# Twelve early rows instead of eight, and half of the weights' low parts on GpSimd

## The reference: what is computed

```python
def peer(h, w_pq, sub_keys, u_tab, v_tab):
    qr = (h @ w_pq).reshape(b, t, 8, 2, 128)                       # queries: 2048 x 2048 weights
    sc = einsum('bthpd,hpnd->bthpn', qr, sub_keys)                 # 8 heads x 2 x 128 scores
    s_top, i_top = top_k(sc, 16)
    cand = s_top[..., 0, :, None] + s_top[..., 1, None, :]
    c_top, c_pos = top_k(cand.reshape(b, t, 8, 256), 16)           # 16 experts for each head
    expert = i0 * 128 + i1                                         # one of 16384
    g = softmax(c_top)
    a = gelu(einsum('bthkd,btd->bthk', u_tab[expert], h))
    return einsum('bthk,bthkd->btd', g * a, v_tab[expert])
```

## Time and profile before

| | us |
|---|---|
| median of 3 runs | 1524.09 (1523.74 to 1526.22) |
| the profiled execution, in all | 1527.39 |
| its span, first to last instruction | 1525.4 |
| PE busy in the span | 1448.7 (95%) |
| VectorE busy | 1153.4 (76%) |
| GpSimd busy | 428.1 (28%) |

### The profile page before, as it was taken

One profiled execution on the slowest core, in us unless ns is written; L12 is line 12 of the kernel. 1 busy time (PEld: TensorE's weight loads), 2 busy tenths in 40 slices (PEclk: granted clock), 3 DMA queues, 4 the chain that ended last, 5 costly groups with the idle time before them and its releaser, 6 DMA issues.

```text
span 1525.4 us, 21815 instructions
## 1 busy us (share of the span) xinstructions
PE 1448.7 (95%) x7977; PEld 1099.6 (72%) x7977; DVE 1153.4 (76%) x1797; ACT 486.7 (32%) x1402; POOL 428.1 (28%) x422
## 2 busy tenths in 40 slices
PE   8999999999999999999989999998887999999995
PEld 6767888888899999999989999973333344444442
DVE  5425688576686899998377777787666898888988
ACT  6646656764654200000144444466000000000000
POOL 2020000000001332223111111135554566666661
PEclk9999999999999999999999999999999999999998
DMA  9764544637679899999999999999999999999996
GB/s 346 276 133 114 164 134 140 206 129 249 199 241 375 339 412 422 421 422 421 422 421 422 420 423 421 422 410 418 418 416 416 392 382 402 403 391 359 405 400 231
DMA packets 115527, 516.23 MB, mean 338 GB/s; under 512 B 26112, under 2 KB 28288, under 8 KB 63312
## 3 DMA queue, kind: packets, MB, share of 16 engines
q0 software_dynamic: 57776, 294.93, 48.9%
q1 hardware_dynamic: 47888, 154.09, 28.3%
q10 hardware_dynamic: 9792, 66.35, 10.5%
HBM read 628.91 MB, written 3.41 MB: 415 GB/s over the span
## 4 chain that ended last, share of the span: by engine, by line
PE 49%; DMA 26%; DVE 18%; issue 3%; ACT 1%; POOL 1%; another core or an unknown queue 0%; DVEq 0%; POOLq 0%; ACTq 0%; SPq 0%
PE ps L1589 12%; PE ps L1634 10%; DMA acts<-in_v_tab,acts 9%; PE ps L1373 6%; PE ps L1378 6%; PE ps L1375 6%; DMA late<-in_u_rows,sel 5%; DVE ps L1195 3%; DMA late<-in_v_tab,acts 3%; DVE late L1186 3%; DMA late<-in_u_tab 2%; PE ps L1395 2%; DVE acts L1186 2%; DMA raw<-in_w_pq 2%; DMA acts<-in_u_rows,sel 2%
## 5 line engine op out<-in xcount | busy, mean ns | idle before, releaser
L871 DVE TENSOR_TENSOR w_lo<-raw,w_hi 128x512 fp32r<-128x512 f32 (+1 forms) x288 | 187.6, 682 | 132.4 <-ACT w_hi L564 131.1
L1589 PE MATMUL ps<-acts,late 128*128 128x128 f32 x1984 | 233.9, 277 | 9.0 <-DMA late<-in_u_tab 7.2
L1589 PEld LDWEIGHTS ps<-acts,late 128*128 128x128 f32 x1984 | 227.1, 193 | 13.1 <-ACT acts L777 6.6
L1589 PE MATMUL ps<-acts,raw 128*128 128x128 f32 x1984 | 231.8, 276 | 2.6 <-DMA raw<-in_u_tab 2.3
L1589 PEld LDWEIGHTS ps<-acts,raw 128*128 128x128 f32 x1984 | 225.5, 192 | 5.3 <-DMA raw<-in_u_tab 3.1
L564 ACT ACTIVATE w_hi<-raw 128x512 fp32r<-128x512 f32 (+1 forms) x288 | 169.4, 621 | 89.3 <-PE ps L1378 35.5
L1634 PE MATMUL ps<-raw,acts 128*128 128x512 f32 x352 | 163.2, 617 | 18.8 <-DMA raw<-in_v_tab,acts 17.5
L1195 DVE SCALAR_TENSOR_TENSOR ps<-acts,sel,ps 128x2048 f32<-128x2048 f32 x63 | 148.3, 2355 | 20.1 <-DMA acts<-in_v_tab,acts 13.8
L1195 DVE SCALAR_TENSOR_TENSOR ps<-late,sel,ps 128x2048 f32<-128x2048 f32 x63 | 148.3, 2355 | 17.6 <-DMA late<-in_v_tab,acts 10.4
L1634 PE MATMUL ps<-late,acts 128*128 128x512 f32 x336 | 150.9, 598 | 10.2 <-DMA late<-in_v_tab,acts 9.5
L1634 PE MATMUL ps<-acts 128*128 128x512 f32 x336 | 150.2, 597 | 5.7 <-DMA acts<-in_v_tab,acts 4.9
(11 more groups left out here) (225 smaller groups left out, 1949.0 us busy)
## 6 DMA issues: line engine op xcount, KB each, us to landing
raw<-in_w_in SPq DMA_DIRECT2D x72, 512.0 KB, 4.4
raw<-in_u_tab SPq DMA_DIRECT2D x32, 1024.0 KB
late<-in_u_tab SPq DMA_DIRECT2D x32, 1024.0 KB
raw<-in_u_tab ACTq DMA_DIRECT2D x30, 1024.0 KB
late<-in_u_tab ACTq DMA_DIRECT2D x30, 1024.0 KB
raw<-in_w_o SPq DMA_DIRECT2D x32, 512.0 KB, 3.7
raw<-in_w_pq SPq DMA_DIRECT2D x32, 512.0 KB, 4.7
acts<-in_u_tab SPq DMA_DIRECT2D x4, 1024.0 KB, 9.1
```

The lines of the kernel that those rows point to most:

```text
L871: V.tensor_tensor(wlo[slot_no][:, 0:w], raw[j % NRAW][:, half * w:half * w + w], whi[slot_no][:, 0:w].bitcast(F32), ALU.subtract).then_inc ...
L1589: ins = mm(ps[:, q, 0:N_DN], unit[:, k * P:k * P + P], hF[:, k, :], start=k == 0, stop=k == KD - 1)
```

## The change

GpSimd makes the low part of the second (odd) piece of each tile from tile 8 on, 24 in all, counted on a semaphore of its own (`odd_lo_done`); VectorE makes the first ones. TensorE, and SyncE before it reloads a buffer, wait for the counts of both. VectorE does twelve row products in the stage (`R_FRONT`), placed by `ROW_AT` after its low parts of tiles 17, 17, 19, 21, 21, 23, 25, 25, 27, 29, 29 and 31; GpSimd's gathers stand at `GATHER_AT`, after its low parts of tiles 14, 15, 18, 18, 20, 22, 22, 24, 26, 26, 28 and 30. During the first top-16 choice VectorE makes a low part at every other step. Expert units 3 and 2 are fetched after the first and second half of `w_o`'s tiles; units 0 and 1 stay where they were. The constants that count rows later on are each raised by four, so that at every later place VectorE and GpSimd stand four rows further.

```diff
-        ROWS_U = 88
-        R_FRONT, R_MORE, ROWS_PICKED = 8, 46, 39
+        ROWS_U = 92
+        R_FRONT, R_MORE, ROWS_PICKED = 12, 50, 43
+        SHARED = 16
+        ROW_AT = [17 + 2 * (2 * r // 3) for r in range(R_FRONT)]
+        GATHER_AT = [14, 15] + [at + 1 for at in ROW_AT[:-2]]
...
-        ROWS_SB = 81
+        ROWS_SB = 85
...
             for group in range(2):
                 with sp.Fori(0, D // 512) as n:
...
+                sp.wait_ge(y_mm, 8 * group + 8)
+                first_unit(3 - group)
...
+                for u in range(4 * first, 4 * end):
+                    sp.wait_ge(lo_done, 2 * B_PQ + SHARED + u + 1 - NRAW - SHARED // 2)
+                    sp.wait_ge(odd_lo_done, u + 1 - NRAW - SHARED // 2)
+                    sp.dma_start(raw[u % NRAW], io["w_pq"][u * P:u * P + P, :]).then_inc(raw_ready[u % NRAW], 16)
...
             first_unit(1)
-            query_weights(4, 5)
-            first_unit(2)
-            query_weights(5, 6)
-            first_unit(3)
-            query_weights(6, 8)
+            query_weights(4, 8)
...
-            gathers(0, R_FRONT + 6)
+            gathered = 0
+            for u in range(SHARED // 2, U_PQ):
+                pool.wait_ge(hi_done, 2 * (B_PQ + u) + 2)
+                part = (2 * u + 1) % NPART
+                nc.gpsimd.tensor_tensor(wlo[part][:, :], raw[u % NRAW][:, PIECE:2 * PIECE], whi[part][:, :].bitcast(F32), ALU.subtract).then_inc(odd_lo_done, 1)
+                end = sum(at <= u for at in GATHER_AT)
+                gathers(gathered, end)
+                gathered = end
+            gathers(gathered, R_FRONT + 6)
...
-                    split_lo_half(B_PQ + lo_halves[0] // 2, lo_halves[0] // 2, lo_halves[0] % 2)
-                    lo_halves[0] += 1
+                    split_lo_half(B_PQ + lo_halves[0] // 2, lo_halves[0] // 2, 0)
+                    lo_halves[0] += 2
...
             while lo_halves[0] < 2 * U_PQ:
-                for _ in range(4):
-                    weights_low()
-                if rows_done[0] < R_FRONT - 1:
-                    next_row()
+                weights_low()
+                next_row(sum(at < lo_halves[0] // 2 for at in ROW_AT) - rows_done[0])
             next_row(R_FRONT - rows_done[0])
...
-                pe.wait_ge(lo_done, 2 * B_PQ + piece + 1)
+                if piece < SHARED:
+                    pe.wait_ge(lo_done, 2 * B_PQ + piece + 1)
+                elif half:
+                    pe.wait_ge(odd_lo_done, (piece - SHARED + 1) // 2)
+                else:
+                    pe.wait_ge(lo_done, 2 * B_PQ + SHARED + (piece - SHARED) // 2 + 1)
```

More of the change, by code:

```diff
@@ L229, in build_block @@
         raw_ready = [sem(f"raw_ready{i}") for i in range(NRAW)]
-        hi_done, lo_done, piece_used = sem("hi_done"), sem("lo_done"), sem("piece_used")
+        hi_done, lo_done, odd_lo_done, piece_used = sem("hi_done"), sem("lo_done"), sem("odd_lo_done"), sem("piece_used")
         xT_in = [sem(f"xT_in{i}") for i in range(KD // 2)]
@@ L403, in _, with u_unit, first_unit @@
             wo = io["w_o"].rearrange("(k p) n -> p k n", p=P)
+            def u_unit(v):
+                return io["u_tab"][ds(v * P, P), :]
+            def first_unit(j):
+                sp.dma_start(first_units[j], u_unit(j)).then_inc(first_in[j], 16)
             for group in range(2):
@@ L408, in _ @@
                         load(n * 4 + (B_WO + 16 * group + j), j, wo[:, k:k + 2, ds(n * 512, 512)])
-            def u_unit(v):
-                return io["u_tab"][ds(v * P, P), :]
+                sp.wait_ge(y_mm, 8 * group + 8)
+                first_unit(3 - group)
             def query_weights(first, end):
[L413 to L418, removed]
+                if first < 3:
+                    with sp.Fori(first, end) as i:
+                        for j in range(4):
+                            load(i * 4 + (B_PQ + j), j, io["w_pq"][ds(i * (4 * P) + j * P, P), :])
+                    return
+                for u in range(4 * first, 4 * end):
+                    sp.wait_ge(lo_done, 2 * B_PQ + SHARED + u + 1 - NRAW - SHARED // 2)
+                    sp.wait_ge(odd_lo_done, u + 1 - NRAW - SHARED // 2)
+                    sp.dma_start(raw[u % NRAW], io["w_pq"][u * P:u * P + P, :]).then_inc(raw_ready[u % NRAW], 16)
             query_weights(0, 3)
@@ L424, in _ @@
             first_unit(1)
-            query_weights(4, 5)
-            first_unit(2)
-            query_weights(5, 6)
-            first_unit(3)
-            query_weights(6, 8)
+            query_weights(4, 8)
             for j in range(2):
-                sp.wait_ge(lo_done, 2 * (B_U + 2 * j + 1) - 2 * (NRAW - 1))
+                sp.wait_ge(lo_done, 2 * B_PQ + SHARED + U_PQ - SHARED // 2 - 2 + 2 * j)
+                sp.wait_ge(odd_lo_done, U_PQ - SHARED // 2 - 2 + 2 * j)
                 sp.dma_start(ring[j], u_unit(NRING + j)).then_inc(unit_in[j], 16)
@@ L1224, in row_numbers, with low_by_turns @@
                 V.scalar_tensor_tensor(idx[:, cols], slot[:, 0, cols], float(NKEY), slot[:, 1, cols], ALU.mult, ALU.add).then_inc(idx_ready, 1)
+            calls = [0]
+            def low_by_turns():
+                calls[0] += 1
+                if calls[0] % 2:
+                    weights_low()
             for hp in range(N_AHEAD):
-                top_k(0, hp, weights_low)
+                top_k(0, hp, low_by_turns)
                 row_numbers(hp)
-            weights_low()
             weights_low()
```

## The result

The changed kernel takes 1527.34 us in the median of its runs (1524.97 to 1531.15), the kernel before 1524.26 on the same chips: a ratio of 1.0016 (95% interval 1.0009 to 1.0023), **2.4 us slower** (the two medians lie 3.1 us apart). One further execution, of 2449 us at a granted clock of 0.556, is left out of the ratio. Forecast were 1532.5, 8.4 us slower: the sign was right, the size about three times too large. The profiled execution took 1527.71 us, with a span of 1525.9.

The account below looks back on a forecast made before the run. TensorE bounds the query stage, the DMA engines (about 421 GB/s) what follows. A start 13.1 us late less 4.6 for four rows gives +8.5 on 1524.1: 1532.6, stated as 1532.5, range 1520 to 1542.

Parts of the forecast that it names:

- four rows fewer later: v stage: 36 of 128 u rows left instead of 40, u stage unchanged; -4.6 us, bounds -2.4 and -10.0.
- the far bound: v stage: all four moved rows' bytes count in full, 4 x 2.49 = -10.0 us.
- the pace: v stage: units without u rows beside them cost 3.61 us each, taken as PE's own speed.
- The late start: End of the query stage: expert units start 13.1 us late, on the path in full.
- The row chain: Query stage: two row buffers, so row r waits for product r-2; PE 13.1 us late; chance 0.62 as forecast.
- early units: w_o stage: fetching expert units 2 and 3 there costs 0, at most 2.49 us of weight delay per fetch.
- a sign of being wrong: Query stage: gather landings of 6 us or less in the trace after would show the forecast wrong.
- The turns: Query stage: two rows cost one landing, a product (2.29) and 0.28 to the next gather; 10.97 us taken.
- The shared port: Query stage: VectorE and GpSimd exclude each other, 3.61 us per tile against PE's 3.10; +4.3, about 1524; chance 0.06.
- the 3.3 us of lead: Query stage: tile 30's first low part was early by this before the change (502.19 against 505.51).
- GpSimd's low part: Query stage: 1.2 us each, between 0.43 and 1.30, so GpSimd keeps up with PE at cost 0.
- u stage: Stage after the query stage: as long as before, with 80 gathers in it before and after.

Follow-up runs that it names:

- e1: The kernel before with the bytes of rows 88 to 91 left out (64 bytes per partition fetched instead), query stage untouched: 1512.27 us, ratio 0.9917.
- e8: The kernel before with expert units 2 and 3 fetched in the w_o stage and nothing else changed: 1525.53 us, ratio 1.0002.
- e2: The kernel before with the first expert unit's matmuls done three times more ahead of the u stage, no row moved: 1534.23 us, ratio 1.0069.
- e12: The changed kernel with a third row buffer, GpSimd still making half of the low parts, products behind the same tiles: 1524.23 us, ratio 0.9994.
- e13: The changed kernel with three row buffers and twelve products spread singly, GpSimd still making half of the low parts: 1521.7 us, ratio 0.9982.
- e10: The changed kernel with three row buffers, all low parts on VectorE, twelve products spread singly: 1516.76 us, ratio 0.9950.
- e14: The changed kernel with three row buffers and all low parts on VectorE, twelve products in pairs behind the same tiles: 1516.64 us, ratio 0.9950.
- e4: The changed kernel with early units 2 and 3 fetched in the query stage, as before the change: 1529.77 us, ratio 1.0031.

## Why the prediction was right and wrong

- **The v stage, the step that failed.** The term "four rows fewer later" was forecast at -4.6; measured are -11.9 in the v stage, -10.8 with the u stage, and -11.7 in e1. The working split the stage at the end of the u rows. Its first part was right: -13.2 forecast (29.8 units at 4.60 against 27.4 at 4.52), -13.1 measured. Its second part charged 2.4 more units at 3.61 us, "which is PE", +8.7; measured is +1.3 (345.2 to 346.5 us, from the border to the end). The first v product of VectorE marks the border, at 1180.25 before and 1179.44 after. PE's matmuls of the stage on both sides of it, before and after (length, busy PE and PEld, clock, DMA share, GB/s):

```profile
1015.65:1180.25 164.60, 137.64 (x292) 55.95 (x293) 0.96 1.02 417
1180.25:1510.00 329.75, 319.09 (x734) 137.53 (x732) 1.00 0.98 385
```
```profile
1027.97:1179.44 151.47, 126.58 (x276) 52.00 (x277) 0.98 1.02 417
1179.44:1510.00 330.56, 324.99 (x750) 140.81 (x748) 1.00 0.99 388
```

  Behind the border PE does 750 matmuls in place of 734, two units more, in the same time, with 5.6 us of idle time instead of 10.7 (3.0 and 2.0 of it behind its last matmul). Its waits for transfers there, before and after:

```profile
PE ps L1634 <- DMA late<-in_v_tab,acts: 2.9, 6, 1.3
PE ps L1634 <- DMA acts<-in_v_tab,acts: 2.4, 3, 1.2
...
PE ps L1634 <- DMA raw<-in_v_tab,acts: 0.7, 1, 0.7
```
```profile
PE ps L1662 <- DMA late<-in_v_tab,acts: 2.5, 3, 1.4
PE ps L1662 <- DMA raw<-in_v_tab,acts: 0.4, 1, 0.4
```

  The added units went where PE had waited for transfers, 6.0 us before and 2.9 after. The row that should have told it stood in the prediction: in the earlier trace rows two units take 7.03 us, 3.515 each, so 21.68 us for six units were not PE's own pace but 0.1 us per unit of something else, and the earlier trace rows have the DMA digit at nine there. So the stretch was held by transfers, not by PE's pace, and four rows count in full, at least the 10.0 us of their bytes (4 x 2.49). That value stood in the working as the far bound and was set aside for the pace. e1 shows that the bytes alone are worth it. Only 2.9 us of such waits are left in the second part after, so moving still more rows might not count in full there; no run here tests it. Why it is 11 to 12 and not 10.0 is not settled: the second part runs at some 390 GB/s, where a row takes 2.7 us, which would make 10.8.
- **The late start.** Forecast 13.1, measured 11.3 in the two profiled executions. It is a little more in fact: against e1 and e8, whose front is that of before or nearly so (510.8 and 510.4), it is 12.4 to 12.8, and from the times an estimate is 13.5 (2.4 us slower, and 11.1 given back by four rows). So this term came out close to its forecast, and the v stage is what made the sum three times too large. That it counts in full is right (e2).
- **Why it is late.** That the number came out close is in part luck. The row chain was one of two sufficient causes. Row 10 began at 513.73, 2 us ahead of the 515.7 of the working, and the 0.9 us of the early units, which were priced at 0, came on top. The landings of the even rows for which VectorE waited were 5.62 to 8.17 us, below the 8.4 taken; two of them, 5.62 and 5.64 (rows 2 and 10), are under the 6 us that the prediction named as a sign of being wrong, but the five landings that make up the turns (rows 0 to 8) average 7.1. The turns were shortened by less, 9.2 to 11.4 us and 10.4 on average against 10.97, since products were stretched to as much as 3.3 us and a gather stood behind GpSimd's low part. The shared port, given a chance of 0.06 as the bound, "lies inside the chain's waits" as long as the chain is there, and takes its place when it is gone (e12, e13). Its price was too small: 4.3 us of late start forecast, 7.7 (e13 against e10; 7.0 by the length of the query stage) and 9.1 (e12 against e14) measured. A tile with a product was priced about right (4.18 us taken, 3.90 in e13). The working averaged over tiles with and without one; if only the twelve with a product are late, 0.80 us each, and the 3.3 us of lead come off, an estimate is 6.3, near e13. No run here tests this.
- **GpSimd's low part.** Taken as 1.2 us, measured 1.29 to 1.31 alone and up to 3.08 beside a product. GpSimd kept up with PE: PE waited for VectorE, not for GpSimd.
- **Early units.** Taken as 0 with a bound of 2.49 each; PE waits 0.9 us once. Left where they were, they made the start 4.4 us later in the profiled execution of e4.
- **u stage.** Unchanged, as forecast (504.8 against 503.7).
- **Slips of the working.** Two, which change nothing: the gather of the earlier trace rows ended 0.81 us after the product of the earlier trace rows, not 0.85, and the sum gives 1532.6, not 1532.5.

## What to carry to other kernels

Where the DMA share stands near 1.0 to the end, price a moved transfer by its bytes, and check a stretch that looks bound by an engine against that engine's own duration per piece of work before charging its pace for what moves into it. Before giving an idle engine a share of work, ask whether it shares a port with the engine relieved: in e13 GpSimd's low parts held VectorE up by more than they took from it. And where two causes are each enough to make a stage late, undoing either shows little; only the run that undoes both finds the gain.

## What the runs showed of the hardware

- GpSimd subtracts two 128 x 512 operands in 1.29 us, VectorE in 0.69. Beside VectorE's products, either engine's instruction counts its wait for the other in its own duration (3.08 and 3.18 us): no idle time shows it.
- A wait of TensorE cost more than itself: behind a slice in which PE was busy 6.90 of 10 us, with a wait of 3.39 us at its end, the granted clock of the next 10 us was 0.68, part of them at 1.2 GHz.
- A gather of 1 MB landed in 5.6 to 8.6 us (the change) though its bytes take 2.49 us at the full rate. With a third buffer VectorE's waits for rows fell from 19.1 us to 2.0 (e12), and with all low parts on VectorE and single products to none (e10).
